# Output-gate panel of mLSTM as seven block products, merged affine steps, and weights after token rows

## The reference, cut to what matters

```
proj = einsum('btd,de->bte', x, w_in[l])              # 14 panels of 256 columns, OB the last in the kernel's order
yb = sigmoid(ob) * head_norm(h, g, True)              # mLSTM; ob is the panel OB
yc = silu(gc) * head_norm(y, g, True)                 # retention
yd = silu(gd) * head_norm(y, g, False)                # HGRN2, y linear in q = silu(qd)
ya = h * gelu(ga)                                     # RG-LRU
out = einsum('bte,ed->btd', concat([ya, yb, yc, yd]), w_out[l])
# layer 1: gates = top 2 of softmax(x @ router)
y = sum over e of gates[e] * (silu(x @ w1[e]) * (x @ w3[e])) @ w2[e]
```

## Time and profile before

| | us |
|---|---|
| median of 3 runs | 992.02 (990.93 to 992.07) |
| the profiled execution | 989.77 |
| its span in the trace | 988.0 |
| PE busy | 964.2 (98%) |
| DVE busy | 506.0 (51%) |
| mix of layer 0, PE | 1 to 154 |
| dense channel mixer | 188 to 423 |
| mix of layer 1, PE | 437 to 573 |
| output projection of layer 1 | 573 to 603 |
| router, first expert | 603 to 651 |
| experts 1 to 7 | 656 to 971 |

### The profile page before, as it was taken

One profiled execution on the slowest core, in us unless ns is written; L12 is line 12 of the kernel. 1 busy time (PEld: TensorE's weight loads), 2 busy tenths in 40 slices (PEclk: granted clock), 3 DMA queues, 4 the chain that ended last, 5 costly groups with the idle time before them and its releaser, 6 DMA issues.

```text
span 988.0 us, 24097 instructions
## 1 busy us (share of the span) xinstructions
PE 964.2 (98%) x10860; PEld 714.7 (72%) x10860; DVE 506.0 (51%) x1025; ACT 190.4 (19%) x402; POOL 81.4 (8%) x105
## 2 busy tenths in 40 slices
PE   9999999999999999999999999979999999999995
PEld 6898877999999999988988788434444444444442
DVE  6989894856556744368988966220101201010135
ACT  1434251321111100143342514100000000000001
POOL 1120124300000000000001100230000020000020
PEclk9999999999999999999999999989999999999998
DMA  9437358124454145211343497999999999999972
GB/s 361 151 118 250 128 180 331 65 86 175 168 203 171 50 186 208 86 44 43 112 142 120 172 373 271 397 339 391 401 424 403 422 389 416 422 423 368 421 285 80
DMA packets 37501, 241.46 MB, mean 244 GB/s; under 512 B 5009, under 2 KB 8145, under 8 KB 17681
## 3 DMA queue, kind: packets, MB, share of 16 engines
q1 hardware_dynamic: 27280, 216.69, 55.5%
q0 software_dynamic: 6432, 19.43, 5.5%
q10 hardware_dynamic: 3680, 3.74, 1.2%
HBM read 228.60 MB, written 13.07 MB: 245 GB/s over the span
## 4 chain that ended last, share of the span: by engine, by line
PE 83%; DVE 10%; DMA 3%; ACT 2%; issue 1%; POOL 1%; DVEq 0%; POOLq 0%
PE ps L776 61%; PE ps L1407 15%; PE ps L1515 6%; DMA expert_tokens<-tables,slot_index 1%; DMA mix_or_moe<-expert_tokens 1%; PE ps L779 1%; DVE small L2489 1%; PE ps L1344 1%; ACT overlay L1864 1%; DMA up_slots<-in_w_in 1%; POOL expert_tokens L735 0%; DVE overlay L2536 0%; ACT up_slots L1864 0%; DVE overlay L2451 0%; DVE mix_or_moe L2449 0%
## 5 line engine op out<-in xcount | busy, mean ns | idle before, releaser
L776 PE MATMUL ps<-up_slots,mix_or_moe 128*32 128x352 f32 (+2 forms) x3248 | 239.0, 454 | 5.0 <-DVE mix_or_moe L3140 5.0
L776 PEld LDWEIGHTS ps<-up_slots,mix_or_moe 128*32 128x32 f32 (+2 forms) x3248 | 100.1, 112 | 138.2 <-issue 116.9
L776 PE MATMUL ps<-x,up_slots 128*128 128x144 f32 (+3 forms) x832 | 151.6, 336 | 0.0
L776 PEld LDWEIGHTS ps<-x,up_slots 128*128 128x128 f32 x832 | 124.9, 190 | 23.1 <-issue 6.0
L776 PE MATMUL ps<-overlay,tables 128*32 128x256 f32 (+3 forms) x1972 | 117.7, 376 | 1.8 <-DVE mix_or_moe L2777 1.1
L776 PEld LDWEIGHTS ps<-overlay,tables 128*32 128x32 f32 (+2 forms) x1972 | 66.5, 113 | 50.4 <-issue 2.9
L3158 DVE TENSOR_TENSOR mix_or_moe<-mix_or_moe,ps 128x352 f32<-128x352 f32 x24 | 11.2, 515 | 173.7 <-PE ps L776 173.7
L1407 PE MATMUL ps<-overlay,up_slots 128*128 128x144 f32 x704 | 91.7, 286 | 0.6 <-DVE overlay L2934 0.3
L1407 PEld LDWEIGHTS ps<-overlay,up_slots 128*128 128x128 f32 x704 | 88.3, 190 | 1.1 <-issue 0.8
L776 PE MATMUL ps<-up_slots 128*128 128x144 f32 (+2 forms) x960 | 79.0, 256 | 1.2 <-DVE up_slots L2570 1.2
L776 PE MATMUL ps<-overlay,up_slots 128*128 128x128 f32 (+3 forms) x528 | 78.2, 308 | 0.0
(11 more groups left out here) (379 smaller groups left out, 987.2 us busy)
## 6 DMA issues: line engine op xcount, KB each, us to landing
up_slots<-in_moe_w SPq DMA_DIRECT2D x64, 1408.0 KB, 17.2
overlay<-in_moe_w SPq DMA_DIRECT2D x21, 1536.0 KB, 15.6
up_slots<-in_ffn_w SPq DMA_DIRECT2D x30, 1024.0 KB, 6.9
up_slots<-in_w_in SPq DMA_DIRECT2D x27, 1024.0 KB, 4.9
up_slots<-in_w_out SPq DMA_DIRECT2D x8, 1024.0 KB, 7.5
overlay<-in_moe_w SPq DMA_DIRECT2D x7, 1024.0 KB, 17.5
mix_or_moe<-in_states POOLq DMA_DIRECT2D x6, 512.0 KB, 4.9
expert_tokens<-in_shape_tables POOLq DMA_DIRECT2D x8, 384.0 KB, 8.7
```

The costliest lines, as they stand in the source:

```text
L776: return pe.matmul(o, lhsT, rhs, start=start, stop=stop)
```

## The change: what it does, and the diff

Panel OB joins `SEVEN` as entry 8 and is computed in two pieces around the last `head_scale`; its four block sums stand around the HGRN2 reciprocal on DVE. The output panels 1 and 2 of each layer are loaded after entry 8 instead of after entry 7. The head variances of HGRN2 and retention are put in 144 columns (the two token halves in two halves of the 32 rows of a head), so that square root and reciprocal take 144 columns instead of 288; the spreading has twice the products of half the width. Scale-and-shift steps are folded into neighbouring operations (`x*0.5+0.5` then `*y` becomes `(x+1)*y`; the halves are taken up in the norm gains, in an epsilon or in a later factor). Three copies out of PSUM move from DVE to ScalarE (ACT). On ACT the exponentials of decay level 3 move ahead of the wait for `mb` and of two evictions. In the MoE, SP waits for all scattered rows before it issues the W1 pairs of expert 1 and, behind these, parts 0 and 2 of the first W2.

```diff
-SEVEN = (4, 5, 6, 7, 9, 10, 11, 12)
+SEVEN = (4, 5, 6, 7, 9, 10, 11, 12, 13)
...
@@ SP, mix
                 sp.wait_ge(*seven_group("sx_pe", l, 6, 2))
-                dense_in(13)
+                seven_in(8)
                 sp.wait_ge(*seven_group("sx_pe", l, 7, 2))
-                for u in range(3):
+                refill(2, ("out", l, 0), w_out[l][0])
+                sp.wait_ge(*seven_group("sx_pe", l, 8, 2))
+                for u in range(1, 3):
                     refill(2 + u, ("out", l, u), w_out[l][u])
@@ SP, MoE
             sp.wait_ge(S["x_ready"], 6 * KT - 2)
-            first_down_part(0)
-            first_down_part(2)
+            sp.wait_ge(S["rows_sent"], 96)
             for e in range(1, NE):
                 up_weights(W1_PAIR, w1_full, w1, e, S["u1_step"])
+                if e == 1:
+                    first_down_part(0)
+                    first_down_part(2)
...
                 up_weights(W3_PAIR, w3_full, w3, e, S["u3_step"])
@@ PE, mix
                 need("ret_ac", "sq")
-                head_var(B_, SQ_RET, "ret_ps")
+                head_var_halves(B_, SQ_RET, "ret_ps")
                 need("hg_dv", "rr")
-                head_scale(C_, RR_HG, "hg_ps")
-                proj_tile(26)
+                head_scale_halves(C_, RR_HG, "hg_ps")
+                seven(8, 0, 3)
                 need("ret_dv", "rr")
-                head_scale(A_, RR_RET, "ret_ps")
-                proj_tile(27)
+                head_scale_halves(A_, RR_RET, "ret_ps")
+                seven(8, 3, 7)
@@ ACT, mix
                 seven(0, 0)
+                level(3)
                 need("gate_ps", "mb")
                 end(f(IS, PS[:, 2:4, 0:NS], ACT.Copy), "gate_ac", "mb")
                 seven(0, 1)
                 seven(0, 2)
-                level(3)
...
+                need("hg_ps", "out")
+                end(f(Y_HG, PS[:, 4:6, 0:T], ACT.Copy), "hg_ac", "y")
@@ DVE, mix
                 def gelu_out():
                     need("th_ac", "ga")
-                    link(ts(GELU, GELU, 0.5, 0.5, M, AD))
-                    link(tt(GELU, GELU, ga, M))
-                    end(tt(mixed[:, 0:2], mixed[:, 0:2], GELU, M), "mixed", "A")
+                    link(stt(GELU, GELU, 1.0, ga, AD, M))
+                    end(stt(mixed[:, 0:2], mixed[:, 0:2], 0.5, GELU, M, M), "mixed", "A")
...
                 last_outputs(6)
+                panel_sums(8, (0, 1))
                 head_rstd(RR_HG, SD_HG, "hg_dv")
+                panel_sums(8, (2, 3))
                 need("th_ac", "GD")
-                link(ts(TH_D, TH_D, 0.5, 0.5, M, AD))
-                link(tt(TH_D, TH_D, proj[:, GD:GD + 2], M))
+                link(stt(TH_D, TH_D, 1.0, proj[:, GD:GD + 2], AD, M))
                 panel_outputs(7)
...
                 end(tt(mixed[:, 4:6], Y_RET, TH_C, M), "mixed", "C")
+                panel_outputs(8)
                 need("th_ac", "OB")
                 gob = proj[:, OB:OB + 2]
-                link(ts(gob, gob, 0.5, 0.5, M, AD))
-                end(tt(mixed[:, 2:4], Y_ML, gob, M), "mixed", "B")
+                end(stt(mixed[:, 2:4], gob, 1.0, Y_ML, AD, M), "mixed", "B")
```

More of the change, by code:

```diff
@@ L163, in shape_tables @@
     half = HD // 2
-    put("room", np.zeros((P, P)))
+    put("varhalves", np.stack([(r[:, None] * 0 + r[None, 0:HR] // (HR // 2) == i) / HD for i in range(2)], 1))
+    put("room", np.zeros((P, P - 2 * HR)))
     pos = np.concatenate([np.arange(SEQ), PAST + np.tile(np.arange(DSEQ), NB)]).astype(np.float32)
@@ L1259, in mix @@
                 seven(5, 0, 3)
-                need("hg_dv", "keys")
+                need("hg_ac", "keys")
                 for c in range(2):
@@ L2002, in mix @@
                 need("lru_dv", "decay")
-                f(a_[:, :, 0:WC], r_[:, :, 0:WC], ACT.Exp)
-                end(f(h_[:, :, 0:WC], r_[:, :, 0:WC], ACT.Tanh), "lru_ac", "decay")
+                need("lru_ac", "tanh")
+                for dst, fn in ((a_, ACT.Exp), (h_, ACT.Tanh)):
+                    for p in range(2):
+                        c = LC[:, 2 * l + p:2 * l + p + 1]
+                        last = f(dst[:, p, 0:WC], r_[:, p, 0:WC], fn, scale=c, bias=c)
+                end(last, "lru_ac", "decay")
                 seven(3, 1)
@@ L2009, in mix @@
                 need("lru_dv", "om")
-                end(f(om_[:, :, 0:WC], om_[:, :, 0:WC], ACT.Sqrt, scale=-1.0), "lru_ac", "sqrt")
+                end(f(om_[:, :, 0:WC], om_[:, :, 0:WC], ACT.Sqrt, scale=-0.25), "lru_ac", "sqrt")
                 for i, (tile_at, landed) in enumerate(((KC, S["swap_k_in"]), (QC, S["swap_q_in"]))):
@@ L2031, in mix @@
                 seven(4, 2)
+                need("hg_ps", "keys")
+                f(KTK[:, 0, 0:2, :], PS[:, 4, :].rearrange("p (t c) -> p t c", t=2), ACT.Copy)
+                end(f(SAMPLE_KEYS[0], PS[:, 5, 0:HD], ACT.Copy), "hg_ac", "keys")
                 seven(5, 0)
@@ L2059, in mix @@
                 end(f(TH_C, proj[:, GC:GC + 2], ACT.Tanh, scale=0.5), "th_ac", "GC")
-                tile(26)
-                tile(27)
+                for g in range(3):
+                    seven(8, g)
                 act.wait_ge(*ev(OB + 1, l))
@@ L2252, in halve_biases @@
             def halve_biases():
-                for name in ("lru_br", "lru_bi"):
-                    link(ts(vec[name], vec[name], 0.5, None, M))
+                for first, last in (("lru_br", "lru_bi"), ("mlstm_norm_g", "hgrn_norm_g")):
+                    columns = VE[:, VEC[first][0]:VEC[last][0] + VEC[last][1]]
+                    link(ts(columns, columns, 0.5, None, M))
             def residual(m, c, bank, evicted):
@@ L2400, in lru_decay @@
                     need("lru_ac", "tanh")
[L2401 to L2405, removed]
-                    link(tt(ig, ig, xc_[:, :, 0:WC], M))
+                    end(stt(ig, ig, 1.0, xc_[:, :, 0:WC], AD, M), "lru_dv", "decay")
                 def lru_gain():
@@ L2746, in mix @@
                 panel_sums(5)
-                need("hg_ps", "keys")
-                cp(KTK[:, 0, 0:2, :], PS[:, 4, :].rearrange("p (t c) -> p t c", t=2))
-                end(cp(SAMPLE_KEYS[0], PS[:, 5, 0:HD]), "hg_dv", "keys")
                 keys(2, 1, "ret_dv")
@@ L2771, in mix @@
                 panel_sums(7)
-                need("ret_ps", "out")
-                end(cp(Y_RET, PS[:, 2:4, 0:T]), "ret_dv", "y")
                 need("hg_ps", "states")
```

65 lines of the change are left out of this document (39 added, 26 removed).

## The result

The changed kernel takes 995.7 us (median of 12 runs) where the kernel before, run beside it, takes 991.5: ratio 1.0047, interval 1.0033 to 1.0061. The forecast was 992.4 us, 0.04% above the median it started from and thus "no change"; the measured time lies inside the range, but the kernel is slower by more than the measurement can hide. The profiled execution took 995.18 us (span 993.3), 5.4 more than that of before.

A forecast was written before the change was run, and what follows sets the result against it. PE, busy 98%, was taken as the bound, with full DMA engines a second one in the MoE. Layer 0 -0.40, layer 1 +1.10, MoE -0.3 put +0.4 on 989.77; 2.25 more for the median gave 992.4 us, range 987.5 to 996.0.

The forecast's parts named there:

- Level 3: Both layers' mixes: with ACT's exponentials ahead of the wait for `mb`, PE's 0.35 us wait for DVE goes in each layer.
- Panel OB: Seven products instead of dense tiles: 0.1 us a layer gained, bounds 0 and 0.95; PE waits 1.1 at second head scaling.
- `p2` in layer 1: Ahead of `p2`, the later output panel delays DVE's sums and copy: PE waits 1.4 us, signal included 1.5.
- Output panels in layer 0: Panels 1 and 2 behind entry 8: PE's first panel, 11.80 us, covers a landing of 4.8; no cost taken.
- Weights behind rows: MoE hold ahead of expert 1: rows land about 631, 7.5 us transfer loss against 7.9 slack; -0.3 us taken.
- the sign "940 to 941": Last expert, expert 7: the landing time of W3 that would show the forecast right.
- the 6.98 us: Expert 1: PE time freed by removing the 4.96 us stall and slow clock, returning as waits in experts 1 to 7.
- Rival A: The forecast: expert 1's stall goes, held weights take the gain back in later experts; 992.4 us, chance 0.46.
- B: MoE: transfers have more room, PE keeps half or all of the 6.98 us; 989.2 or 985.7 us, chance 0.27.
- D: MoE: the last scatter's 13.9 us are its own, rows land at 641 as before; about 1003 us, chance 0.04.
- C: MoE: the held queue loses more than the slack, rows late, perhaps one long wait and slow clock; 996.9 us, chance 0.23.
- The scatter's price: MoE, last scatter without weights beside it: 4 us to land, bounds 2.9 to 5.6.

The follow-up runs named there:

- f3: d3 with deviations and reciprocals in 288 columns and wide spreading products again, 64 records fewer: 991.1 us, ratio 1.0001.
- b2: The kernel before, with GpSimd's SwiGLU weight sums begun after the second output panel of layer 0 instead of the first: ratio 1.0044.
- a4: The changed kernel with SP's MoE order as before the change, no wait for the rows and W2 parts first: ratio 1.0037.
- d1: The kernel before plus SP's wait for the scattered rows ahead of W1 of expert 1, the two W2 parts behind W1: ratio 1.0008.
- a1: The changed kernel with panel OB dense again and all three output panels loaded behind entry 7, as before: ratio 1.0024.
- a3: The changed kernel with parts 0 and 2 of the first W2 issued behind W3 of expert 1 instead of ahead of it: ratio 1.0066.
- f1: The kernel before, with PE's four starting products of ones each split into nine narrower ones, 64 records more, same columns: 1001.3 us.
- d3: The changed kernel without panel OB by seven products and without the wait for the rows: 986.0 us, ratio 0.9955.
- e2: d3 with SP issuing W1 of expert 1 only when parts 0 and 2 of the first W2 have landed: 985.8 us.

## Why the prediction was right or wrong

- **Level 3.** Expected 0.35 us a layer; PE's offset against before falls by 0.41 in layer 0 and 0.42 in layer 1. Right.
- **Panel OB.** Expected 0.1 us a layer and a wait of 1.1 us at the second head scaling; between the head mean and the output projection 0.23 a layer is won, and the wait is 0.80. DVE's chain takes back what PE saves, as put.
- **`p2` in layer 1.** Expected 1.5 us; 1.51. Right, in place and size.
- **Copies and merged steps.** Taken at nothing. f3 has them and the earlier level 3, but neither panel OB, hold nor halved deviations, and the stall as before: ratio 1.0001 (0.9988 to 1.0014). Nothing to be seen, and level 3's 0.8 us is within the interval too.
- **Output panels in layer 0: this is the step that failed.** "Behind this wait in SP's queue lie the loads that follow; they have tens of microseconds" was asked only of PE. The SwiGLU panels behind it feed GpSimd's sums, and their slip of 4.4 us beyond PE's own put them beside DVE's folds: 2.46 us of PE, and b2 shows it in the kernel before at 4 us. In the sum the price was taken at nothing with PE's first panel as cover; whom the late load feeds, and what that engine then lies beside, was not followed. The Trainium skill, "SBUF — State Buffer", section "SBUF: two separate sides", has DVE operations with two SBUF inputs and GpSimd operations take a port pair that they share as an exclusive lock, for a whole instruction. The trace agrees: the fold of 0.46 us takes 2.48 beside a GpSimd sum of 2.86.
- **Weights behind rows.** The rows' landing was put at 631 in the clock of before; it is 636.5 less the shift of 5.8, 630.7. The loss of 7.5 us against a slack of 7.9 was right too: W3 of the last expert lands at 952 (922 and 30.1 us), when PE needs its last pair at 951.9. (In the clock of before that is 946.3; the sum's own terms give 938.9 + 7.5 = 946.4, and the sign "940 to 941" did not follow from them.) Gain expected 0.3 us, in the profiles 0.5, by a4 and d1 none within 0.2%. Where the 6.98 us go was half right: not in waits over experts 1 to 7 but in one of 4.61 us at W3 of expert 1 with 1.7 us of slow clock, because the two W2 parts stand ahead of it. Rival A stands for the MoE; B and D did not come, and of C neither the late landing nor the long wait in the last expert.
- **The scatter's price** was taken at 4 us, and is 3.6 (636.51 less 632.88). By the rule of the Trainium skill, "DMA: Bandwidth & Descriptors", section "Anatomy of one DMA — SWDGE (gpsimd) path", it would have been 2.3, an estimate. The measurement, with the scatters before it on the same queue, lies 1.3 above that and 2.0 below the row of 5.6; the price put between them was good.
- **What no step named.** The prediction took the stall of 4.96 us as the weights' doing, since the scatter lay beside them. They are a part of it: with nothing queued (changed, a1, a3, d1) the scatter takes 3.5 to 4.6 us. But f1 shows that the same weights in the same order leave no stall when PE's program is 64 records longer.
- **Two more parts of the 5.4 us** between the two profiles lie in the mix of layer 0. 0.8 us are at the start, as in the second profile of the kernel before: the first gate products take 1.18 us instead of 0.68; the windows give the granted clock as 1.00 there in both, so the reason stays open. 1.8 us are at the rotated queries, where DVE waits 1.75 us for a panel in the one profile and not in the other, and PE then 1.72 us instead of 0.43. Kernels of the same mix differ as much there (0.4 before and 1.7 in b2, 0.6 in d3 and 1.7 in e2), so no single profile ties it to the change; but the 1.7 stands in four of the seven traces with OB by block products and in two of the thirteen others, so a part of it may be the change's. That is open.

So the sum missed by the folds: with their 2.5 us it would have said 0.4 + 2.5 = 2.9 us slower. The measured difference is 3.3 to 6.0; where the remaining 0.4 us or more lie is not shown.

## What to carry to other kernels

Ask of every load behind a new wait not only when PE needs it but which engine works on it first, and what that engine's work will then lie beside. Where transfers bound a stretch, a hold that frees one of them is paid by the last; find its slack before counting a stall as a gain. And before a stall at the mercy of transfers is repaired by an order of loads, move the code by some inert records: here 64 were worth 6.6 us of the MoE, and the hold nothing. They are a test and no repair: where they were put they cost 14 us themselves.

## What was not expected of the hardware

Whether a scatter of 128 KB takes 8 or 14 us hangs on 64 inert records of PE far ahead of it. The place of one instruction fetch, a packet of 0.02 MB, goes with it in all eleven traces without the hold; that the fetch itself is the cause is argued. The Trainium skill, "Runtime: NRT & Kernel Launch", section "Instruction fetch mechanics", has the refill come in blocks of 256 instructions and calls its cost mostly hidden. The trace agrees with the block, about: a packet per 123 records, each a weight load and a product. If the fetch is the cause, its cost here was not hidden but 6.6 us.

While token rows are read from DRAM beside the weights the DMA engines are as busy as ever and move less: in the changed kernel share 0.99 and 340 GB/s at 670 to 675, when GpSimd's queue moves 0.20 MB in 100 packets, with 428 GB/s in the next window, which has none of them, at share 1.03.

```profile
670.00:675.00 5.00, 0.97 (x16) 0.19 (x7) 0.00 (x0) 1.18 (x3) 0.00 (x0) 1.00 0.99 340
```
